# Turning feed-forward activations in 32x32 blocks through VectorE and device memory instead of through TensorE

## The reference

```python
def swiglu_ffn(x, w_gu, w_down):
    a, u = jnp.split(x @ w_gu, 2, axis=-1)
    return (jax.nn.silu(a) * u) @ w_down

x = layer_norm(DEEPNORM_ALPHA * x + 0.5 * swiglu_ffn(x, ffn1_w_gu[l], ffn1_w_down[l]),
               ln1_g[l], ln1_b[l])
```

## Time and profile before

| | |
|---|---|
| median of 3 runs | 1331.56 us (1330.89 to 1331.66) |
| span of the profiled execution | 1328.9 us, 2.7 us under that median |
| TensorE busy, weight load busy | 99%, 84% |
| VectorE busy | 77% |
| ScalarE busy | 51% |
| granted TensorE clock | 0.998 |
| DMA | 264.92 MB, mean 199 GB/s |

### The profile page before, as it was taken

How to read it: one execution, slowest core, us unless ns; L and a number is a source line. 1 busy time by engine, 2 the same in 40 slices (tenths; PEclk the granted TensorE clock), 3 DMA queues, 4 the chain that set the end, 5 groups by cost and what they waited for, 6 DMA issues and landing times.

```text
span 1328.9 us, 18838 instructions
## 1 busy us (share of the span) xinstructions
PE 1311.6 (99%) x7096; PEld 1110.0 (84%) x7096; DVE 1019.8 (77%) x1625; ACT 675.3 (51%) x1069; POOL 105.4 (8%) x153
## 2 busy tenths in 40 slices
PE   9999999999999999999999999999999999999997
PEld 7888888788888888888887888888889998798995
DVE  6677778887777677777787887778676798966986
ACT  6444444644444344444446545444436667457672
POOL 1010100011011001111010011111000000000000
PEclk9999999999999999999999999999999999999999
DMA  8977756527767656776646358777646473463630
GB/s 268 326 232 229 226 187 208 142 96 246 244 228 233 222 185 219 223 236 228 236 161 202 102 173 292 231 253 235 221 142 200 146 237 129 143 214 118 203 128 32
DMA packets 195049, 264.92 MB, mean 199 GB/s; under 512 B 17232, under 2 KB 140240, under 8 KB 194448
## 3 DMA queue, kind: packets, MB, share of 16 engines
q1 hardware_dynamic: 183248, 223.12, 52.1%
q0 software_dynamic: 11712, 40.60, 8.9%
HBM read 262.61 MB, written 1.07 MB: 198 GB/s over the span
## 4 chain that ended last, share of the span: by engine, by line
PE 87%; DVE 7%; DMA 4%; ACT 1%; issue 1%; SPq 0%; DVEq 0%; ACTq 0%
PE ps L818 26%; PE ps L820 26%; PE ps L819 26%; PE ps L902 4%; DVE w_lo L1317 2%; DMA w_raw<-in_ffn_w_gu 2%; PE ps L1049 2%; DMA w_raw<-in_w_in 1%; PE ps L1084 1%; PE ps L1110 1%; DVE few_first L1346 1%; ACT w_hi L1141 1%; DVE y L1345 1%; PE ps L1018 0%; PE ps L1096 0%
## 5 line engine op out<-in xcount | busy, mean ns | idle before, releaser
L1317 DVE TENSOR_TENSOR w_lo<-w_raw,w_hi 128x1024 fp32r<-128x1024 f32 (+2 forms) x420 | 496.9, 1213 | 128.5 <-ACT w_hi L1141 126.5
L1141 ACT ACTIVATE w_hi<-w_raw 128x1024 fp32r<-128x1024 f32 (+2 forms) x420 | 431.0, 1053 | 247.9 <-DMA w_raw<-in_ffn_w_gu 122.0
L818 PE MATMUL ps<-w_hi,col_hi 128*128 128x512 f32 (+2 forms) x1024 | 396.7, 387 | 3.6 <-DVE w_lo L1324 1.4
L820 PE MATMUL ps<-w_hi,col_lo 128*128 128x512 f32 (+2 forms) x1024 | 392.0, 383 | 0.0
L819 PE MATMUL ps<-w_lo,col_hi 128*128 128x512 f32 (+2 forms) x1024 | 391.9, 383 | 0.0
L818 PEld LDWEIGHTS ps<-w_hi,col_hi 128*128 128x128 f32 x1024 | 192.6, 188 | 44.0 <-DVE w_lo L1317 4.3
L820 PEld LDWEIGHTS ps<-w_hi,col_lo 128*128 128x128 f32 x1024 | 192.5, 188 | 38.2
L819 PEld LDWEIGHTS ps<-w_lo,col_hi 128*128 128x128 f32 x1024 | 192.5, 188 | 34.6
L818 PE MATMUL ps<-w_hi,lat_hi 128*128 128x512 f32 (+2 forms) x544 | 208.8, 384 | 0.0
L820 PE MATMUL ps<-w_hi,lat_lo 128*128 128x512 f32 (+2 forms) x544 | 206.5, 380 | 0.0
L819 PE MATMUL ps<-w_lo,lat_hi 128*128 128x512 f32 (+2 forms) x544 | 206.3, 379 | 0.0
(11 more groups left out here) (148 smaller groups left out, 1172.8 us busy)
## 6 DMA issues: line engine op xcount, KB each, us to landing
w_raw<-in_ffn_w_gu SPq DMA_DIRECT2D x352, 256.0 KB, 4.5
w_raw<-in_w_in SPq DMA_DIRECT2D x108, 512.0 KB, 4.6
w_raw<-in_ffn_w_down SPq DMA_DIRECT2D x88, 512.0 KB, 4.9
mod<-in_w_ada POOLq DMA_DIRECT2D x32, 768.0 KB, 7.6
w_raw<-in_w_out SPq DMA_DIRECT2D x24, 512.0 KB, 4.5
norm_g<-in_ln_g POOLq DMA_DIRECT2D x8, 512.0 KB, 4.2
norm_b<-in_ln_b POOLq DMA_DIRECT2D x8, 512.0 KB, 6.1
w_raw<-in_w_out SPq DMA_DIRECT2D x16, 256.0 KB, 4.5
```

Source lines behind the costliest of these rows:

```text
L818: pe.matmul(dst, a_hi, b_hi, start=start, stop=False)
L820: return pe.matmul(dst, a_lo, b_hi, start=False, stop=stop)
L1141: act.activation(half_of(w_hi[j], n, h), half_of(raw[j], n, h), ACT.Copy).then_inc(hi_ready, 1)
L1317: tt(half_of(w_lo[j], n, h), half_of(raw[j], n, h), half_of(w_hi[j], n, h).bitcast(F32), ALU.subtract)\
```

## The change

For all rounds but the last of a stage, `ht(r)` is taken away. In its place:

- `hturn(r)`, right behind gu(r,1): VectorE turns `hidden` of both token tiles in one instruction in 32x32 blocks, from one part of the buffer `arena` to another (`h_blocks`).
- On SyncE, behind the load of the unit that takes the place of gu(r,1)'s last: wait for that turn, and one DMA of 256 KB from `h_blocks` to device memory (`h_stage`). Behind the load of the next unit: wait until it is stored, and four DMAs of 64 KB, one for each partition group of 32, back to `h_cols`. That puts the blocks where a full transpose would have them.
- `hparts(r)`, where `ht(r)` stood or a little later: ScalarE makes `lat_hi` in two copies of 128x256, once all four loads have landed, and VectorE makes `lat_lo` in two subtractions of 128x256. `down(r)` waits for these.
- `hmove(r)` is in the list only so that counts are right; no engine does anything for it.

```diff
@@ def ffn_jobs(s):
+    blocks, moved, parts = (lambda r, kind=kind: [(kind, s, r)] for kind in ("hturn", "hmove", "hparts"))
     if s == 0:
...
-        jobs += gu(1, 0)[:1] + [("ht", s, 0)] + gu(1, 0)[1:] + [("params", s)] + gu(1, 1)
+        jobs += blocks(0) + gu(1, 0)[:1] + moved(0) + gu(1, 0)[1:] + parts(0) + [("params", s)] + gu(1, 1) + blocks(1)
     else:
...
-        jobs += gu(1, 0)[1:] + gu(0, 1) + [("params", s)]
-        jobs += gu(1, 1)[:1] + [("ht", s, 0)] + gu(1, 1)[1:]
+        jobs += gu(1, 0)[1:] + gu(0, 1) + blocks(0) + [("params", s)]
+        jobs += gu(1, 1)[:1] + moved(0) + gu(1, 1)[1:] + blocks(1) + parts(0)
     for r in range(2, ROUNDS):
-        jobs += gu(r, 0) + [("ht", s, r - 1)]
+        if r == 2:
+            jobs += gu(r, 0)[:1] + moved(1) + gu(r, 0)[1:]
+        else:
+            jobs += gu(r, 0)
+        jobs += parts(r - 1)
...
         jobs += gu(r, 1)
+        if r < ROUNDS - 1:
+            jobs += blocks(r)
...
+def moves_behind(n):
+    s, name = UNITS[n - SLOTS] if n >= SLOTS else (0, ("", 0))
+    return (s, name[1]) if name[0] == "gu" and name[2] == 1 and name[1] < ROUNDS - 1 else None
...
@@ SyncE, behind the loads of unit n
+                move = moves_behind(n - 1)
+                if move is not None:
+                    sp.wait_ge(h_stored, 16 * at["hturn", move])
+                    if at["hturn", move] > 1:
+                        sp.wait_ge(h_split, at["hturn", move] - 1)
+                    sp.sem_inc(s_marks, 1)
+                    for b in range(4):
+                        sp.dma_start(h_cols[32 * b:32 * b + 32, :, :], h_stage[:, :, b, :].rearrange("a f n -> f a n"))\
+                            .then_inc(h_moved, 16)
+                move = moves_behind(n)
+                if move is not None:
+                    sp.wait_ge(h_turned, at["hturn", move])
+                    if at["hturn", move] > 1:
+                        sp.wait_ge(h_moved, 64 * (at["hturn", move] - 1))
+                    sp.sem_inc(s_marks, 1)
+                    sp.dma_start(h_stage.rearrange("a f b n -> (a f) b n"), h_blocks).then_inc(h_stored, 16)
@@ ScalarE
+                elif kind == "hparts":
+                    act.wait_ge(h_moved, at["hmove", (s, r)])
+                    if r >= 4:
+                        act.wait_ge(used, NUMBER[s, ("down", r - 4)] + 1)
+                    act.activation(h_part(lat_hi, q)[:, 0], h_as_columns[:, 0], ACT.Copy)
+                    act.activation(h_part(lat_hi, q)[:, 1], h_as_columns[:, 1], ACT.Copy).then_inc(hi_part, 1)
@@ VectorE
+                elif kind == "hturn":
+                    dve.wait_ge(hidden_done, at["hidden", (s, r, 1)])
+                    if at["hturn", (s, r)] > 1:
+                        dve.wait_ge(h_stored, 16 * (at["hturn", (s, r)] - 1))
+                    dve.transpose(h_blocks.rearrange("p b (c t) -> p b c t", t=32),
+                                  hidden[:, r % 2, :, :].rearrange("p i (g b f) -> p b (i g) f", g=2, b=4)).then_inc(h_turned, 1)
```

More of the change, by code:

```diff
@@ L182, in ffn_jobs @@
         jobs += gu(r, 1)
+        if r < ROUNDS - 1:
+            jobs += blocks(r)
         if lag < ROUNDS - TAIL:
-            jobs += down(lag, 0) + down(lag, 1)
+            jobs += down(lag, 0) + moved(r) + down(lag, 1)
             lag += 1
+        elif r < ROUNDS - 1:
+            jobs += moved(r)
         if r < 2 + MOD_STEPS:
@@ L453, in count_jobs @@
                     ENDS["sums", s, tile] = ENDS[group]
-        if kind in ("xt", "ht", "trlat", "ycols"):
+        if kind in ("xt", "ht", "hparts", "trlat", "ycols"):
             COUNT.add("hi_part", job)
+        if kind in ("hturn", "hparts"):
+            COUNT.add(kind, job[1:])
+        if kind == "hmove":
+            COUNT.add(kind, job[1:], 4 * 16)
         if kind == "ycols" and not TURN[job]:
@@ L640, in build @@
         hidden = arena[:, 512:1536].rearrange("p (r t n) -> p r t n", r=2, t=TT)
+        h_blocks = arena[:, 1536:2048].rearrange("p (b n) -> p b n", b=4)
+        h_cols = arena[:, 2048:2560].rearrange("p (a n) -> p a n", a=4)
         rows1 = arena[:, 0:TT * IN1].rearrange("p (t n) -> p t n", t=TT)
@@ L671, in build @@
         gain_gate = mod[:, 2 * D:3 * D]
+        h_stage = nc.dram_tensor("hidden_blocks", (4, 32, 4, P), F32, kind="Internal").ap()
         def shift_scale(s):
@@ L710, in build @@
          weighed, y_cols, ret_mixed, half_sum, var_ready, rstd_ready, h_ready, x_ready, y_ready, rope_done, rotated, idx_w_ready,
-         idx_summed, rope_a_done, rope_k_done, squares, latent, folded, mod_summed, mod_hi, mod_lo, mod_row) = (
+         idx_summed, rope_a_done, rope_k_done, squares, latent, folded, mod_summed, mod_hi, mod_lo, mod_row,
+         h_turned, h_moved, h_split, h_stored) = (
             sem(n) for n in ("group_done", "silu_done", "hidden_done", "copied", "hi_part", "scores", "score_free", "maxed",
@@ L714, in build @@
                              "h_ready", "x_ready", "y_ready", "rope_done", "rotated", "idx_w_ready", "idx_summed",
-                             "rope_a_done", "rope_k_done", "squares", "latent", "folded", "mod_summed", "mod_hi", "mod_lo", "mod_row"))
+                             "rope_a_done", "rope_k_done", "squares", "latent", "folded", "mod_summed", "mod_hi", "mod_lo", "mod_row",
+                             "hidden_blocks_turned", "hidden_blocks_moved", "hidden_split", "hidden_blocks_stored"))
         x_in = [[sem(f"x_landed{i}{h}") for h in range(2)] for i in range(TT)]
@@ L747, in sink_of, with h_part @@
             return sinks.rearrange("p (f j) -> p f j", f=2)[:, :, pairs[0]:pairs[-1] + 1]
+        def h_part(tile, q):
+            return tile[:, q:q + 2, :].rearrange("p g (i a t) -> p g i a t", i=TT, a=4)
+        h_as_columns = h_cols.rearrange("p a (i g t) -> p g i a t", i=TT, g=2)
         def sum_banks(s, i):
@@ L948, in _ @@
                     r, i = job[2:]
-                    turns_done(("ht", s, r))
+                    if r < ROUNDS - 1:
+                        pe.wait_ge(h_split, at["hparts", (s, r)])
+                    else:
+                        turns_done(("ht", s, r))
                     q = 2 * (r % 4)
@@ L1191, in _ @@
                         .then_inc(hi_part, 1)
+                elif kind == "hparts":
+                    r = job[2]
+                    q = 2 * (r % 4)
+                    act.wait_ge(h_moved, at["hmove", (s, r)])
[3 more added lines that the diff above has]
+                    act.activation(h_part(lat_hi, q)[:, 1], h_as_columns[:, 1], ACT.Copy).then_inc(hi_part, 1)
                 elif kind == "T":
@@ L1400, in _ @@
                     if r >= 2:
-                        b, n = TURN["ht", s, r - 2][0]
-                        dve.wait_ge(turned[b], n + 1)
+                        dve.wait_ge(h_turned, at["hturn", (s, r - 2)])
                     dve.wait_ge(silu_done, nth)
@@ L1405, in _ @@
                         ALU.mult, ALU.mult).then_inc(hidden_done, 1)
+                elif kind == "hturn":
+                    r = job[2]
+                    dve.wait_ge(hidden_done, at["hidden", (s, r, 1)])
[3 more added lines that the diff above has]
+                                  hidden[:, r % 2, :, :].rearrange("p i (g b f) -> p b (i g) f", g=2, b=4)).then_inc(h_turned, 1)
+                elif kind == "hparts":
+                    q = 2 * (job[2] % 4)
+                    dve.wait_ge(hi_part, at["hi_part", job])
+                    tt(h_part(lat_lo, q)[:, 0], h_as_columns[:, 0], h_part(lat_hi, q)[:, 0].bitcast(F32), ALU.subtract)
+                    tt(h_part(lat_lo, q)[:, 1], h_as_columns[:, 1], h_part(lat_hi, q)[:, 1].bitcast(F32), ALU.subtract)\
+                        .then_inc(h_split, 1)
                 elif kind == "ht":
```

## The result

The changed kernel takes 1451.44 us in the median of 4 runs (1446.82 to 1452.48), the kernel before 1331.22 us: ratio 1.0897, 95% interval 1.088 to 1.0914. That is 120 us more; the prediction had 30 more (1361, range 1336 to 1390). The direction was right and the size was not.

A forecast was written before the change was run, and what follows sets the result against it. TensorE was taken to bound the kernel, busy 1311.6 of 1328.9 us. The terms -15.1 + 11 + 10.4 + 13.2 + 10 gave +29.5 us, so 1361 us, range 1336 to 1390.

The forecast's parts named there:

- work taken off TensorE: 40 turns leave TensorE, 8 without spread at 0.45 us and 32 with it at 0.36: 15.1 us saved.
- place 1: First rounds of stage 0: loads back land at 44.2 us behind parameter loads, TensorE waits 11 us before gu(2,1).
- place 2: Round 1's activations in every stage: late loads back make TensorE wait 2.6 us at round 3's spread, 10.4 in all.
- place 3: Loop of rounds with modulation: a lap of 17.15 us against TensorE's 16.6, 0.55 us each, 13.2 in all.
- place 4: Last turn of each stage: round 9's loads back wait behind a unit, TensorE waits 2.5 us, 10 in 4 stages.
- place 5: Last spread of each stage, waiting for the modsplit behind round 9's turn; the prediction had no such term.
- direct cost: VectorE's turn 0.6 to 0.69 us, parts with hand-over about 1.6 us on VectorE and ScalarE; called small.
- D: In each lap, end of VectorE's turn to landing of the loads back: about 8.0 us, least 6.2, upper bound 9.2.
- the loop is wider: Rival: store and the 768 KB chunk delay the weights too, lap 18.35 us, total 1390 us; 15 in 100.
- six laps a stage: Laps counted as costing: turns 3 to 8, setting the spread of rounds 4 to 9; 3.3 us a stage.
- all hidden: Rival: loads back get past the weights, no place costs anything, 1316.5 us; 8 in 100.

The follow-up runs named there:

- e1: Changed kernel without its round trip: no store or loads back, lat_hi and lat_lo read VectorE's turned blocks directly, outputs not the reference's; 1315.59 us.
- e6: Changed kernel with the store and four loads back issued by GpSimd at hmove's place, SyncE loading weights alone; 1490.89 us.
- e7: Changed kernel with SyncE issuing the four loads back directly behind the store, ahead of the next unit of weights; 1375.95 us.
- e8: Changed kernel with the changes of e3 and e7 together; 1382.34 us.
- e3: Changed kernel with the parts of round r-1 moved behind turn, down and modulation of round r, half a round later; 1337.68 us.
- e11: Changed kernel with 1 of the 7 multiply-adds of each modsum on VectorE, transfers unchanged; 1391.2 us.
- e5: Changed kernel with the last spread and its modrow behind gu(10,1) instead of ahead of it; 1448.57 us.
- e4: Changed kernel with dummy matmuls on TensorE inside its long waits; 1438.95 us.
- e9: e3 with the four loads back of stage 0, round 0 directly behind their store; 1326.01 us, ratio 0.9966 to the kernel before.
- e2: As e1, but store and four loads back are issued and waited for on SyncE, landing in a buffer nobody reads; 1318.59 us.

## Why the direction was right and the size was not

The account of the 116 us between the spans 1328.9 and 1445.0, term by term. Waits are those of the changed kernel's trace, the work and the clock come from TensorE's busy time in e1:

| term | predicted | measured |
|---|---|---|
| work taken off TensorE | -15.1 | -17.0 (busy 1311.6 to 1294.6 in e1) |
| place 1 | 11 | 13.6 |
| place 2 | 10.4 | 13.5 (1.7 + 3.8 + 4.0 + 4.1) |
| place 3, laps | 13.2 | 40.2 (56.2 + 21.9, less places 2 and 5) |
| place 4 | 10 | 13.6 |
| place 5, round 9 to 10 | 0 | 24.4 (5.4 + 6.1 + 5.8 + 7.1) |
| TensorE busy for longer | 0 | 29.6 (1324.2 - 1294.6) |

They add up to 118; the 2 us of difference are not placed.

**Removed work and direct cost: right.** The turn takes 0.711 us (0.69 from the earlier trace rows), the parts' operations 0.42, and e1 shows that they are hidden.

**Places 1, 2 and 4: right in mechanism, low by a fifth to a quarter.** Place 1's landing was put at 44.2 and came at 46.8 us. Place 2's wait stands one job earlier than the prediction had it, at the second half of gu(3,0) (stage 2: 3.8 us at 386.93): a weight split that TensorE needs there stands on VectorE behind the parts and the modulation, like `modsplit`. The Trainium skill, in "DMA: Bandwidth & Descriptors", section "Anatomy of one DMA", gives 2 us fixed plus the bytes for a DMA that GpSimd issues, by which store and loads are 2.6 and 2.2 us as an estimate; measured are 2.3 and 2.2 in GpSimd's queue (e6), 2.1 and 1.9 in SyncE's where nothing is ahead (the lap above; e7 at 343 us), and far more behind weights (the store 4.8 in the median of the changed kernel, 7.8 at 568 us in e8).

**Place 3: the step that failed first.** The prediction put "D", turn to landing, at 8.0 with a bound of 9.2, and took 8.0, "the weights ahead of them in the same queue"; the lap shown above has 9.24. Both of its summands were low: the last of the four weight loads took 6.3 us and not the 5.4 of the earlier trace rows, and the loads back came about 0.9 behind it and not 0.5 (2.0 + 6.3 + 0.9 where 2.1 + 5.4 + 0.5 was summed). The rest of the lap came out to a hundredth: 7.55 + 1.6 = 9.15 predicted, 8.38 + 0.76 = 9.14 measured; that close is luck. But the term is a difference of large numbers, 17.15 - 16.6, and so 1.24 us in D make 1.8 us of each 0.55. The third rival, *the loop is wider*, with a lap of 18.35, was the case; I gave it 15 in 100. Its time, 1390, is still 61 us short, because it has neither of the two terms that follow. e3 and e11 show that it is the loop: the former takes the landing out of it, the latter 2.7 us of VectorE.

**The last lap was left out.** The prediction counted "six laps a stage (turns 3 to 8 set the `spread` of rounds 4 to 9)". Turn 9 stands ahead of `modsplit` too, and the `spread` behind it comes after a round without a `down`, so 5.4 us earlier for TensorE than all others. VectorE, late by the laps before, is waited for with all of it: 24.4 us, a term that the prediction did not have. e5 shows that this is lateness of VectorE and not a wait of the `spread` alone.

**The waits were priced at their own length.** No wait of TensorE in the trace of before is above 1.4 us, its clock hardly falls there, and the prediction had no term for it. The changed kernel has 13 waits of 3.2 us and more, and behind 11 of them the job of 12 matmuls takes 4.3 to 5.5 us from its first start to its last end, where 2.9 is usual; its busy time is 29.6 us above e1. Those 11 jobs make 20.6 us of that. Some 7 more are not the clock: at each wait the matmul ahead of it is counted with its whole 0.39 us and not with the 0.23 to the next start, and the rows above have 46 waits where e1 has 4 (an estimate, 42 x 0.16). e4 shows cause and direction, and gives back 12.5 us. The Trainium skill, in "TensorE: Matmul & The Clock Gate", section "Part 1: The HAM clock gate (the "warmup" mystery)", has the two levels and says that idleness brings the lower one; the starts 0.43 and 0.23 us apart agree with its 1.2 and 2.4 GHz. By it a sum of waits without such a term is too low; by how much, only the rows here say.

**Of the rivals**, *all hidden* describes e1 exactly: 1316.5 against 1315.6 measured, but only without the transfer. With the transfer and another order (e9) a third of its gain is reached, 5.1 of 15.1 us; e9 is still 10 us above e1, with 6.5 us of waits at `spread` and TensorE busy for 4.3 us more. That another order could be had was not considered.

Open: whether the one late place of e2 comes from the bytes or from SyncE's waits, by both of which it differs from e1; the 1.7 us at the `spread` of round 3 that e3 and e9 keep; and the 1.5 us between landing and next issue on GpSimd, of which the trace says only "issue".

## What to carry to other kernels

When a transfer is put between two engines, write down the whole cycle through their programs, not the latency: if the thing that starts the transfer stands behind the thing that waits for it, the latency is paid in every round. Moving the waiter behind the starter gave back 114 us here. Where a term is the small difference of two laps, carry its upper bound as the forecast's weight, follow it to the last round, and look where the covering work is missing there. And price a long wait of TensorE at its length plus about 2 us for the slower job behind it (20.6 us over 11 waits here). Last, when a transfer moves to another engine, look at what that engine does next: the transfer was faster there and the kernel 39 us slower, since the load behind it came late.
